# High weights loaded by rounding transfers, and the recurrent gates as three rounded products, in the attention stage of a two-block kernel

## The reference

```python
xb = x.reshape(bsz, s, RNN_BLOCKS, RNN_BLOCK_W)
r = jax.nn.sigmoid(jnp.einsum('bsnc,ncd->bsnd', xb, w_a).reshape(bsz, s, D_RNN) + b_a)
i = jax.nn.sigmoid(jnp.einsum('bsnc,ncd->bsnd', xb, w_x).reshape(bsz, s, D_RNN) + b_x)
log_a = LRU_C * r * jax.nn.log_sigmoid(lam)
a = jnp.exp(log_a)
u = jnp.sqrt(-jnp.expm1(2.0 * log_a)) * (i * x)
```

## Time and profile before

| | |
|---|---|
| median of 3 runs | 811.46 us (811.45 to 811.59) |
| the profiled execution's own time | 811.55 us |
| its span, first to last instruction | 809.8 us |
| granted TensorE clock, mean | 0.997 |
| TensorE busy | 99% |
| VectorE, ScalarE busy | 74%, 60% |
| DMA queues, read from HBM | 141.97 MB |

### The profile page before, as it was taken

The page is one execution under the profiler, slowest core; times in us unless marked ns, Lnnn a source line. Parts: engine busy times, 40 slices in busy tenths (PEclk is TensorE's granted clock), DMA queues, the critical chain, the costliest instruction groups (busy, mean ns, idle before and its releaser), DMA issues.

```text
span 809.8 us, 11913 instructions
## 1 busy us (share of the span) xinstructions
PE 799.9 (99%) x4813; PEld 694.6 (86%) x4813; DVE 599.0 (74%) x773; ACT 486.6 (60%) x738; POOL 27.1 (3%) x38
## 2 busy tenths in 40 slices
PE   9999999999999999999999999999999999999996
PEld 8889998888888888988888888888888888888885
DVE  6774698998958986897878678877777665655556
ACT  6555598877767454665666566546755654544552
POOL 1102000000000000000000000020110000000000
PEclk9999999999999999999999999999999999999998
DMA  8446433342434774456555555664453655465431
GB/s 338 160 159 251 169 126 105 118 155 70 154 119 159 251 266 156 156 197 219 161 204 182 197 193 183 253 240 142 144 197 123 211 198 201 170 220 190 162 151 52
DMA packets 22630, 143.79 MB, mean 178 GB/s; under 512 B 2608, under 2 KB 3248, under 8 KB 8240
## 3 DMA queue, kind: packets, MB, share of 16 engines
q1 hardware_dynamic: 20880, 137.72, 48.0%
q10 hardware_dynamic: 1696, 5.31, 1.9%
HBM read 141.97 MB, written 1.05 MB: 177 GB/s over the span
## 4 chain that ended last, share of the span: by engine, by line
PE 92%; ACT 3%; DVE 3%; issue 1%; DMA 1%; DVEq 0%; SPq 0%; ACTq 0%
PE PS L1749 19%; PE PS L1753 10%; PE PS L1802 10%; PE PS L1803 10%; PE PS L1806 10%; PE PS L1736 5%; PE PS L1737 4%; PE PS L1741 4%; PE PS L2120 2%; PE PS L1765 2%; PE PS L2099 2%; PE PS L1859 1%; PE PS L2124 1%; PE PS L1893 1%; PE PS L1870 1%; PE PS L1773 1%
## 5 line engine op out<-in xcount | busy, mean ns | idle before, releaser
L1075 DVE TENSOR_TENSOR WL<-RAW,WH 128x2048 fp32r<-128x2048 f32 (+2 forms) x127 | 284.6, 2242 | 32.3 <-ACT WH L630 32.1
L630 ACT ACTIVATE WH<-RAW 128x2048 fp32r<-128x2048 f32 (+2 forms) x127 | 238.1, 1877 | 51.3 <-PE PS L1806 26.4
L1491 DVE TENSOR_TENSOR HLS<-PS,HLS 128x512 f32<-128x512 f32 x46 | 31.7, 689 | 92.7 <-ACT HLS L978 92.7
L1749 PE MATMUL PS<-CHL,WH 128*128 128x512 f32 x352 | 87.9, 392 | 0.0
L1736 PE MATMUL PS<-BHL,WH 128*126 128x256 f32 (+1 forms) x336 | 83.8, 287 | 0.0
L978 ACT ACTIVATE HLS<-PS 128x512 f32<-128x512 f32 x46 | 27.4, 595 | 90.8 <-PE PS L1753 86.4
L1737 PE MATMUL PS<-BHL,WH 128*126 128x256 f32 (+1 forms) x336 | 81.8, 282 | 0.0
L1749 PE MATMUL PS<-BHL,WH 128*128 128x512 f32 x320 | 79.9, 392 | 0.0
L1749 PEld LDWEIGHTS PS<-CHL,WH 128*128 128x128 f32 x352 | 63.9, 189 | 11.8
L1803 PE MATMUL PS<-WH,AHL 128*128 128x512 f32 x176 | 68.8, 391 | 0.0
L1802 PE MATMUL PS<-WH,AHL 128*128 128x512 f32 x176 | 68.7, 390 | 0.0
(11 more groups left out here) (313 smaller groups left out, 1312.3 us busy)
## 6 DMA issues: line engine op xcount, KB each, us to landing
RAW<-in_w_stream SPq DMA_DIRECT2D x108, 1024.0 KB, 4.9
RAW<-in_w_stream SPq DMA_DIRECT2D x11, 1008.0 KB, 4.8
RAW<-in_w_stream SPq DMA_DIRECT2D x8, 704.0 KB, 4.7
WF<-in_w_stream SPq DMA_DIRECT2D x2, 1024.0 KB, 5.2
LN<-in_ln ACTq DMA_DIRECT2D x2, 1024.0 KB, 5.1
WF<-in_w_stream SPq DMA_DIRECT2D x4, 294.0 KB, 3.6
X<-in_x SPq DMA_DIRECT2D x2, 512.0 KB, 4.2
RAW<-in_w_stream SPq DMA_DIRECT2D x2, 512.0 KB, 6.6
```

The costliest lines, as they stand in the source:

```text
L630: eng.activation(WH[:, c % NSLOT, 0:CHUNKS[c][2]], raw(c), ACT.Copy).then_inc(w_hi, 1)
L1075: eng.tensor_tensor(WL[:, c % NSLOT, 0:CHUNKS[c][2]], raw(c), f32(WH[:, c % NSLOT, 0:CHUNKS[c][2]]), ALU.subtract).then_inc(w_lo, 1)
L1491: eng.tensor_tensor(HLS[:, n % 4, :, :], PS[:, bank:bank + 2, 0:TOK], HLS[:, n % 4, :, :], ALU.add)\
L1749: eng.matmul(PS[:, bank, :], wh, HL[:, k, :, :].rearrange("p a t -> p (a t)"), start=(k == 0), stop=False)
```

## The change

1. Chunks "ri" are split like the others and count in the RAW slots; their blocks for the crossing products are widened from 42 to 106 columns, with zeros.
2. WH of chunks 17 to 39 (CAST, 23 chunks) is no longer rounded by ScalarE: POOL issues a second transfer from HBM that rounds on the way (fp32 to fp32r), for chunk c + 2 when chunk c - 1 is done. WH of chunk 16 is still rounded by ScalarE.
3. WL of the "ri" chunks, and the low part of each convolution result (AL), are computed on POOL (new semaphore rg_low); the high part (AH) is a copy on ScalarE (rg_round), in the step after the projection.
4. VectorE splits a chunk of CAST one step before its use (chunk c + 1 at step c, ahead of unit_weights) and not two.
5. TensorE makes each gate product of three rounded ones; the crossing products too, now of 42 rows and 106 columns.
6. In the step before the group of three, ScalarE evicts the mixing gate and then the first gate tile ahead of the step's exponentials.

Waits of the other users are renumbered (wait_high in place of the wait for w_hi, LOW_NO in place of SPLIT_NO), and the second block's semaphores up2_* are merged into up_*, counting on.

```diff
-    return RG_TILES[g] * RP + HB
+    return RG_TILES[g] * RP + 64 + HB
...
-        out += [("ri", g, 2 * gate_cols(g), False)]
+        out += [("ri", g, 2 * gate_cols(g), True)]
...
+CAST = [c for c in range(AT[("ri", 0)] + 1, AT[("ao", 3)] + 1) if CHUNKS[c][3]]
...
+GATES3 = AT[("ri", RG_TILES.index(3))]
...
+        def wait_high(eng, c):
+            if c in CAST:
+                n = CAST.index(c)
+                eng.wait_ge(wh_in[n % 2], 16 * (n // 2) + 16)
+            else:
+                eng.wait_ge(w_hi, HI_NO[c] + 1)
+        def wait_both(eng, c):
+            wait_high(eng, c)
+            if c in CAST:
+                eng.wait_ge(raw_in[ARRIVAL[c][0]], 16 * (ARRIVAL[c][2] + 1))
...
@@ sync
-                        eng.wait_ge(w_lo, before + 1)
+                        if CHUNKS[before][0] == "ri":
+                            eng.wait_ge(rg_low, RG_LOW_NO[CHUNKS[before][:2]])
+                        else:
+                            eng.wait_ge(w_lo, LOW_NO[before] + 1)
@@ gpsimd
+            for c in range(NCH):
+                if c + 2 in CAST:
+                    s, n = (c + 2) % NSLOT, CAST.index(c + 2)
+                    source = A_w[OFFS[c + 2]:OFFS[c + 3]].rearrange("(p n) -> p n", p=P)
+                    eng.wait_ge(chunk_done, c)
+                    if n >= 2:
+                        eng.wait_ge(wh_in[n % 2], 16 * (n // 2))
+                    eng.dma_start(WH[:, s, 0:CHUNKS[c + 2][2]], source).then_inc(wh_in[n % 2], 16)
+                if c + 1 < NCH and CHUNKS[c + 1][0] == "ri":
+                    s, n = (c + 1) % NSLOT, CHUNKS[c + 1][2]
+                    wait_both(eng, c + 1)
+                    eng.tensor_tensor(WL[:, s, 0:n], raw(c + 1), f32(WH[:, s, 0:n]), ALU.subtract).then_inc(rg_low, 1)
+                if c and CHUNKS[c - 1][0] == "rnn":
+                    i = CHUNKS[c - 1][1]
+                    G, t = RG_OF[i]
+                    eng.wait_ge(xc_hi, RNN_NO[i] + 1)
+                    eng.tensor_tensor(AL[0:RP, i, :], XC[:, G % 2, t, :], f32(AH[0:RP, i, :]), ALU.subtract).then_inc(rg_low, 1)
@@ scalar
+            def rg_round(i):
+                G, t = RG_OF[i]
+                eng.wait_ge(mb_dve, RNN_NO[i] + 1)
+                eng.activation(AH[0:RP, i, :], XC[:, G % 2, t, :], ACT.Copy).then_inc(xc_hi, 1)
...
+                if c and CHUNKS[c - 1][0] == "rnn":
+                    rg_round(CHUNKS[c - 1][1])
+                if c + 1 == GATES3:
+                    side(c)
+                    gates_out(c + 1, 0, 2)
                 u = unit_at(c - W0)
                 if u is not None:
                     unit_exp(u)
...
-                side(c)
+                if c + 1 != GATES3:
+                    side(c)
@@ vector
-                if c and CHUNKS[c - 1][0] == "ri" and c - 1 != SPLIT_AHEAD or c == UNIT_FIRST:
+                if c + 1 in CAST:
                     split(c + 1)
...
-                if CHUNKS[c][:2] not in SUMS_FIRST and kind != "ri" and c != W0 and c + 1 != UNIT_FIRST or c == SPLIT_AHEAD:
+                if CHUNKS[c][:2] not in SUMS_FIRST and c + 2 not in CAST and c != W0:
                     split(c + 2)
@@ tensor
-                    eng.wait_ge(mb_dve, RNN_THROUGH[i])
+                    eng.wait_ge(rg_low, max(RG_LOW_NO["ri", i], *(RG_LOW_NO["rnn", k] for k in range(RG_AT[i], RG_AT[i + 1]))))
...
+                            rows = wh[0:RP, which, RP * t:RP * t + RP]
+                            eng.matmul(outs[which], rows, AH[0:RP, k, :], start=(which == 0), stop=False, skip_group_check=True)
+                            eng.matmul(outs[which], rows, AL[0:RP, k, :], start=False, stop=False, skip_group_check=True)
+                        for which in range(2):
+                            last = eng.matmul(outs[which], wl[0:RP, which, RP * t:RP * t + RP], AH[0:RP, k, :], start=False,
...
+                        for n, (W, A) in enumerate(((wh, AH), (wh, AL), (wl, AH))):
+                            other = W[:, which, RP * RG_TILES[i]:gate_cols(i)]
+                            ins = eng.matmul(PS[0:64 + HB, banks[0], cols], other[0:HB, 0:64 + HB], A[0:HB, first + 1, :],
...
+                            last = eng.matmul(PS[0:64 + HB, banks[1], cols], other[64:64 + HB, 0:64 + HB], A[64:64 + HB, first, :],
```

More of the change, by code:

```diff
@@ L136 @@
                max(RNN_NO[i] for i in range(RG_AT[g], RG_AT[g + 1])) + 1 for g in range(NG)]
+LOW_NO = [sum(1 for x in CHUNKS[:c] if x[3] and x[0] != "ri") for c in range(NCH)]
+_low_order = []
+for _c in range(NCH):
+    _low_order += [x[:2] for x in CHUNKS[_c + 1:_c + 2] if x[0] == "ri"]
+    _low_order += [x[:2] for x in CHUNKS[max(0, _c - 1):_c] if x[0] == "rnn"]
+RG_LOW_NO = {_k: _n + 1 for _n, _k in enumerate(_low_order)}
 SPLIT_NO = [sum(1 for x in CHUNKS[:c] if x[3]) for c in range(NCH)]
 PLAIN = [c for c in range(NCH) if not CHUNKS[c][3]]
+CAST = [c for c in range(AT[("ri", 0)] + 1, AT[("ao", 3)] + 1) if CHUNKS[c][3]]
+HI_NO = [sum(1 for b in range(c) if CHUNKS[b][3] and b not in CAST) for c in range(NCH)]
 LOAD_ORDER = sorted(range(NCH), key=lambda c: c + (0 if CHUNKS[c][3] else 1.5))
@@ L154, in arrival_slots @@
         out[c] = (slot, last[slot], uses[slot])
-        last[slot] = SPLIT_NO[c]
+        last[slot] = c
         uses[slot] += 1
@@ L622, in split @@
             def split(c):
-                if c >= NCH or not CHUNKS[c][3]:
+                if c >= NCH or not CHUNKS[c][3] or c in CAST:
                     return
@@ L818, in side @@
                     for m in range(ahead, len(order)):
[L819 removed]
+                        gates_out(c, m, order[m])
                 if kind == "ro":
@@ L2063, in main @@
                 if kind == "ri":
-                    eng.wait_ge(mb_dve, RNN_THROUGH[i])
-                    w = plain(c).rearrange("p (a n) -> p a n", a=2)
+                    eng.wait_ge(rg_low, max(RG_LOW_NO["ri", i], *(RG_LOW_NO["rnn", k] for k in range(RG_AT[i], RG_AT[i + 1]))))
+                    wh, wl = (W[:, c % NSLOT, 0:2 * gate_cols(i)].rearrange("p (a n) -> p a n", a=2) for W in (WH, WL))
                     banks = {}
                     for m, t in enumerate(gate_order(i)):
+                        k = RG_AT[i] + t
                         banks[t] = mb_bank(MB_NO[c] + m)
+                        outs = [PS[0:RP, banks[t], 256 * which:256 * which + 256] for which in range(2)]
                         for which in range(2):
-                            last = eng.matmul(PS[0:RP, banks[t], 256 * which:256 * which + 256],
-                                              w[0:RP, which, RP * t:RP * t + RP], XC[:, i % 2, t, :], start=(which == 0),
+                            rows = wh[0:RP, which, RP * t:RP * t + RP]
[3 more added lines that the diff above has]
+                            last = eng.matmul(outs[which], wl[0:RP, which, RP * t:RP * t + RP], AH[0:RP, k, :], start=False,
                                               stop=(t == 2), skip_group_check=True)
@@ L2157, in main @@
                 if kind in ("dn", "dn2"):
-                    first_bank, lo_s, n_all = (2, up_lo, N_UP // 2) if kind == "dn" else (0, up2_lo, N_UP2 // 2)
+                    first_bank, before, n_all = (2, 0, N_UP // 2) if kind == "dn" else (0, N_UP, N_UP2 // 2)
                     def down_half(cc, j, t, n):
@@ L2419, in gates_blocks @@
             first, second = rows_of[0, 64:64 + HB], rows_of[1, 0:HB]
-            out[0:HB, which, n * RP:] = dense[second[:, None], first[None, :]]
-            out[64:64 + HB, which, n * RP:] = dense[first[:, None], second[None, :]]
+            out[0:HB, which, n * RP + 64:] = dense[second[:, None], first[None, :]]
+            out[64:64 + HB, which, n * RP:n * RP + HB] = dense[first[:, None], second[None, :]]
         return out.reshape(P, -1)
```

92 lines of the change are left out of this document (44 added, 48 removed).

## The result

The forecast was 809.3 us, faster; the changed kernel takes **814.17 us** (median of six runs, 813.81 to 815.62) against 811.55 for the kernel before: a ratio of 1.0036, 95% interval 1.0026 to 1.0046. It is slower, by 0.36%, outside the range (808.3 to 813.0), on the side to which I gave 0.19. The profiled execution took 813.91 us, 2.36 more than before's 811.55; its span is 812.2.

A forecast was written before the change was run, and what follows sets the result against it. TensorE, busy in 99% of the span, was taken as the bound. Terms 1.6 + 0.7 + 0.5 - 0.15 - 0.4 = 2.25 us, off the profiled 811.55, gave 809.3; own range 808.3 to 811.3, overall 808.3 to 813.0.

The forecast's parts named there:

- The tiles and the crossing products: Gate groups on TensorE: eleven tiles as rounded products save 1.6 us; crossing products, running in pairs, save 0.7 us.
- Rival 1: Crossing products of the gate groups run one after the other, five groups losing 2.9 us: 812.8 us; chance 0.15.
- The wait in chunk 25: TensorE's 0.83 us wait for VectorE's copy shrinks as a split moves away: 0.5 saved, range 0.83 saved to 1.2 lost.
- The new wait for low parts: Gate group of chunk 20 waits for taps, ScalarE's rounding and POOL's subtraction: 0.4 us lost, range 0 to 2.
- Rival 2: POOL holds VectorE in steps 22 to 24 and 27 to 29, where VectorE is full: 813.4 us; chance 0.17.
- The third tile and the copies: Chunk 20: third tile's wait loses 0.15 us; PT copy, now behind the early eviction, counted at nothing.
- I count nothing: Chunk 20's PT copy: done at 4.2 us after group start, when TensorE needs it; 0.4 lost if ScalarE is late.
- evicting ahead brings nothing: Chunk 20: ScalarE was waiting for TensorE, not late, so evicting ahead of the exponentials gains nothing.
- What moved off the path: ScalarE's lost roundings, its new copies, the queues and POOL's 23 transfers are covered by TensorE: 0 us.
- rival 3: The rounding transfers are slow: if rounding doubles an engine's time, 19 us longer, 830 us; chance 0.08.

## Why the prediction was wrong

- **The tiles and the crossing products: right.** Chunk 16's group takes 2.39 us (98.96 to 101.35) against 2.81, 0.42 for a forecast of 0.43; chunks 30 and 35 take 2.49. The crossing products run in pairs:

```profile
101.23 0.28 PE L2137 MATMUL PS<-AHL,WL 42*106 42x256 f32 x1
101.23 0.28 PE L2139 MATMUL PS<-AHL,WL 42*106 42x256 f32 x1
101.35 1.03 PE L1911 MATMUL PS<-KT,QT 64*128 64x256 f32 x8
```

  Rival 1 is out.
- **The wait in chunk 25: right.** The whole 0.83 is saved, more than the 0.5 I took: the group takes 2.53 (164.59 to 167.12) against 3.75. VectorE was held there as well, 2.1 us, but early enough ahead of the copy. The price came elsewhere: the maximum of chunk 26 was late and TensorE waited 0.7 for its exponentials, 0.8 in the table; with the low weights on VectorE that wait is gone.
- **The new wait for low parts: the step that failed.** I took 0.4 (range 0 to 2) and reasoned that POOL might be held by VectorE's split, behind the taps. The taps themselves were late: I had them end at 120.85, they ended at 123.57, because the instruction ahead of them was held by POOL's own 2.30 us. The group came nearly 2.5 us after it was due. Rival 2, which holds VectorE and gives 813.4, has the mechanism, but places the hold in steps 22 to 24 and 27 to 29; that its time is near is luck, since its losses at chunks 25 and 30 (1.2 and 0.9) did not come. (Its 813.4, like rival 1's 812.8, is counted from the median of 811.46; from the 811.55 that the forecast starts from it is 813.5.) For chunk 20, the one group that I had called tight, I priced no hold of VectorE: POOL's 968 columns of low weights stand in no sum.
- **The third tile and the copies: also wrong.** "I count nothing" for the PT copy was a sum without the 1.28 us of the table load, which the early eviction puts behind the tanh: 4.2 by my sum, 5.5 with it, 5.54 to 5.84 measured. And "evicting ahead brings nothing" holds only while the maximum is early. The third tile itself came out as said: the group at full clock takes 3.61 to 3.69, my sum gave 3.59.
- **What I had no term for: the clock.** The group ran at half clock behind the wait in front of it, and with products in that wait it did not: 1.0 us, of which the PT copy's wait hid most in this kernel and nothing once the copy was early (with the table load ahead the group still takes 4.69, and the products with V follow it without a wait). Which waits bring the clock down is not settled: with the low weights on VectorE, waits of 1.35 and 1.22 us are followed by 0.50 from 130 to 133; with the taps first, waits of 1.0 and 1.2 are not.
- **What moved off the path: right.** No wait of TensorE is for WH; rival 3 is out.

In sum, against the forecast's -2.25: 2.0 more for the low parts, 1.05 for the clock, 0.6 for the PT copy, 0.25 at the softmax weights ahead of the group, 1.0 in chunks 26 and 28, 0.3 better in chunk 25: 4.6, which is the measured difference of 813.91 and 809.3.

The rule of the Trainium skill that I weighed (page "SBUF — State Buffer", section "Who interferes with whom") decided this case: two SBUF inputs on VectorE and a GpSimd instruction that reads SBUF exclude each other for their length, and an instruction with at most one is left alone. The traces agree on both counts: the multiplication (SM and wt) 3.87, the scan (AA and XC) 2.23 instead of 1.22 at 234.43, POOL's low part 1.75 instead of 0.73 at 152.27 beside a split; the taps, with one input in PSUM, kept their 0.48 each, three of them in the row below beside POOL's low weights from 92.66 to 94.42.

```profile
92.53 1.52 DVE L1351 SCALAR_TENSOR_TENSOR XC<-PS,CV,XC 126x255 f32<-126x255 f32 x3 [1.52 <-ACT RGT L852]
```

The forecast's words "whichever is first" do not fit by the recorded starts: the multiplication began 0.49 us ahead of POOL's subtraction (0.48 at 154.08) and was the one held, while POOL took its plain 2.30. Why is not shown.

## What to carry to other kernels

Work given to an idle engine is free only if it shares nothing with a full one: ask for each new POOL instruction which VectorE instruction it will overlap, whether that one has two inputs in SBUF, and count POOL's length on VectorE's queue where that queue is tight. When an eviction is moved ahead on ScalarE, look for the table load that moves behind it, and place a small activation of the next table where ScalarE waits anyway. A new wait of 2 us on TensorE can cost half its clock afterwards, as here, so price it together with the work behind it.

## What was not expected of the hardware

- The exclusion works to the instruction: a VectorE instruction that started half a microsecond before POOL's ended 1.1 us after it, and with two POOL instructions the engines took turns (3.86, 2.72).
- TensorE's clock fell half a microsecond after work had resumed, not in the wait: 1.00 in the empty stretch from 123 to 124.9, 0.50 at 126, back at 129.
- Tanh needed no table load behind the GELU in its tanh form (L777, which had its own load at 114.06; the tanh at 123.93 in the changed kernel had none), nor behind an exponential (123.67 in the kernel with the table load ahead); the exponential behind GELU and tanh did, 1.28 us.
- Two transfers per chunk kept the DMA engines at a share of 0.94 to 1.12 from 119 to 129 us, and no product waited for them.
